# PEER routing tables: fused one-hot products, gates of 48 tiles applied from PSUM, split subtractions moved to GpSimd

## The reference

```python
q = (xn @ w_q).reshape(B, S, 8, 2, 64)
s = einsum('bshpd,hpkd->bshpk', q, sub_keys)          # 8 heads, 2 halves, 128 keys
v_half, i_half = top_k(s, 16)
top_s, top_c = top_k(v_half[..., 0, :, None] + v_half[..., 1, None, :], 16)
experts = i1 * 128 + i2                                # one of 16384, 128 per token
g = softmax(top_s)
act = gelu(einsum('cd,ced->ce', xc, expert_u[experts]))
y = einsum('ce,ced->cd', g * act, expert_v[experts])
```

## Time and profile before

| | us |
|---|---|
| median of 3 runs | 1444.72 |
| lowest, highest | 1444.61, 1446.04 |
| the profiled execution | 1441.05 |
| its span | 1439.2 |
| TensorE busy | 1253.0 (87%) |
| VectorE busy | 1091.7 (76%) |
| ScalarE busy | 720.3 (50%) |
| GpSimd busy | 683.8 (48%) |

### The profile page before, as it was taken

One profiled execution on the slowest core, in us unless ns is written; L12 is line 12 of the kernel. 1 busy time (PEld: TensorE's weight loads), 2 busy tenths in 40 slices (PEclk: granted clock), 3 DMA queues, 4 the chain that ended last, 5 costly groups with the idle time before them and its releaser, 6 DMA issues.

```text
span 1439.2 us, 27850 instructions
## 1 busy us (share of the span) xinstructions
PE 1253.0 (87%) x8802; PEld 1132.1 (79%) x8802; DVE 1091.7 (76%) x1727; ACT 720.3 (50%) x1473; POOL 683.8 (48%) x543
## 2 busy tenths in 40 slices
PE   7979989888978889899877777777899999999996
PEld 6978878777966889898876666666888878888785
DVE  4587777786355539994899999999568777788765
ACT  5435665434555455456433333333445555555554
POOL 2653543432356338999888888888630000000000
PEclk8999999998999999999999999999999999999999
DMA  5575655754534335454354545454777567766652
GB/s 209 169 227 188 204 185 186 249 160 170 206 105 144 112 110 174 156 167 162 121 160 143 159 146 160 146 159 147 234 257 253 190 245 250 249 245 205 236 191 100
DMA packets 98190, 261.92 MB, mean 182 GB/s; under 512 B 7979, under 2 KB 41899, under 8 KB 96844
## 3 DMA queue, kind: packets, MB, share of 16 engines
q1 hardware_dynamic: 90652, 232.76, 48.7%
q0 software_dynamic: 7472, 28.31, 5.8%
HBM read 241.65 MB, written 19.40 MB: 181 GB/s over the span
## 4 chain that ended last, share of the span: by engine, by line
PE 48%; DVE 25%; issue 11%; POOL 7%; ACT 4%; DMA 3%; DVEq 1%; POOLq 0%; ACTq 0%; SPq 0%
PE psum L640 47%; DVE w_lo L1530 8%; DVE arena L1930 7%; POOL w_lo L1400 5%; DVE s_sb L1927 3%; DVE s_sb L1539 2%; POOL arena L1466 2%; DMA ring<-v_rows 1%; ACT w_hi L1068 1%; DMA arena<-mods 1%; DVE arena L1928 1%; ACT arena L1205 1%; PE psum L803 1%; DVE arena L1759 1%; DVE rstd L1524 1%
## 5 line engine op out<-in xcount | busy, mean ns | idle before, releaser
L1068 ACT ACTIVATE w_hi<-ring 128x512 fp32r<-128x512 f32 x734 | 451.7, 629 | 494.5 <-PE psum L640 479.2
L640 PE MATMUL psum<-h_hi,w_hi 128*128 128x256 f32 x1832 | 542.9, 296 | 51.9 <-DVE w_lo L1530 19.6
L1400 POOL TENSOR_TENSOR w_lo<-ring,w_hi 128x512 fp32r<-128x512 f32 x287 | 421.0, 1476 | 279.5 <-ACT w_hi L1068 223.9
L640 PE MATMUL psum<-h_lo,w_hi 128*128 128x256 f32 x1832 | 523.0, 285 | 0.0
L640 PE MATMUL psum<-h_hi,w_lo 128*128 128x256 f32 x1832 | 522.3, 285 | 0.0
L640 PEld LDWEIGHTS psum<-h_hi,w_hi 128*128 128x128 f32 x1832 | 354.8, 194 | 73.4 <-issue 33.8
L1530 DVE TENSOR_TENSOR w_lo<-ring,w_hi 128x512 fp32r<-128x512 f32 x319 | 294.2, 923 | 122.4 <-ACT w_hi L1068 122.2
L640 PEld LDWEIGHTS psum<-h_lo,w_hi 128*128 128x128 f32 x1832 | 356.5, 195 | 0.3
L640 PEld LDWEIGHTS psum<-h_hi,w_lo 128*128 128x128 f32 x1832 | 355.7, 194 | 0.0
L640 PE MATMUL psum<-w_hi,h_hi 128*128 128x512 f32 (+1 forms) x592 | 223.8, 378 | 11.1 <-DVE arena L1547 5.4
L640 PE MATMUL psum<-w_lo,h_hi 128*128 128x512 f32 (+1 forms) x592 | 222.6, 376 | 0.0
(11 more groups left out here) (186 smaller groups left out, 1072.4 us busy)
## 6 DMA issues: line engine op xcount, KB each, us to landing
ring<-u_t SPq DMA_DIRECT2D x128, 512.0 KB, 3.5
ring<-v_rows SPq DMA_DIRECT2D x128, 512.0 KB, 3.5
ring<-weights SPq DMA_DIRECT2D x115, 512.0 KB, 3.7
arena<-mods POOLq DMA_DIRECT2D x48, 512.0 KB, 4.7
routing_weights<-s_sb SPq DMA_DIRECT2D x32, 512.0 KB, 4.8
s_sb<-routing_weights SPq DMA_DIRECT2D x8, 2048.0 KB, 9.2
bias_rows<-arena POOLq DMA_DIRECT2D x1, 1536.0 KB, 5.9
xres<-x_t SPq DMA_DIRECT2D x1, 1024.0 KB, 4.9
```

The lines of the kernel that those rows point to most:

```text
L640: return nc.tensor.matmul(out, lhs, rhs, start=start, stop=stop, **kw)
L1068: nc.scalar.activation(w_hi[:, half, :], src, ACT.Copy).then_inc(hi_done, 1)
L1400: nc.gpsimd.tensor_tensor(w_lo[:, half, :], src, w_hi[:, half, :].bitcast(F32), ALU.subtract)\
```

## The change

It rearranges the routing in four ways.

1. The table of quad q is cut in two. The part for tiles 0 to 47 never leaves PSUM: VectorE multiplies it straight into the 48 activations of these four tokens (`weigh_early`, 192 columns), after which ScalarE copies only the part of tiles 48 to 127 (`late_of`, 320 of 512 columns) to `stage`. HBM holds five groups instead of eight. The first product therefore uses only PSUM banks 0 and 1 in turn, and tile n waits for the gelu of tile n-2; the routing tables take banks 2, 3, 6, 7, as `sel_1` now stays in bank 4.
2. There is no `hot2` any more. The three weighted tables come from twelve `tensor_scalar` per quad on VectorE, each 128 columns: (iota == index) * piece, with both scalars read per partition from SBUF. The pieces are rounded to bf16 and kept as fp32 for that. `hot1` compares against an index column in PSUM.
3. GpSimd makes no tables; it does both low halves of all 128 tiles of the first product, and VectorE none.
4. VectorE's loop over quads is written out in full (64 times), and its weighings in the second product begin with tile 48, at other places of each group.

```diff
-UBANKS = (0, 1, 6, 7)
+UBANKS = (0, 1, 0, 1)
+GBANKS = (2, 3, 6, 7)
+XBANKS = (0, 1, 6, 7)
...
+LATE = (P - POOL_TILES) // GRP
...
-        hot1, hot2 = quads(flat(120, 2)), quads(s_sb[:, 0:512])
-        wgt = [quads(flat(122 + 2 * x, 2)) for x in range(3)]
-
-        sel_w = [s_sb[:, 512 + 128 * x:640 + 128 * x].bitcast(BF16) for x in range(3)]
-        rest = [s_sb[:, 1024 + T * x:1024 + T * x + T] for x in range(2)]
-        sel_1, sel_2 = std, rstd
-        stage = s_sb[:, 2048:4096].rearrange("p (b r t g) -> p b r t g", b=2, r=GROUPS, t=8)
+        hot1 = flat(112, 2).bitcast(BF16).rearrange("p (b t k) -> p b t k", b=2, t=4)
+        wgt = flat(114, 6).bitcast(BF16).rearrange("p (b t x k) -> p b t x k", b=2, t=4, x=3)
+        sel_2 = s_sb[:, 0:T]
+        sel_w = [s_sb[:, T * (x + 1):T * (x + 2)] for x in range(3)]
+        piece = s_sb[:, 1024:1024 + T // 2].bitcast(BF16)
+        rest = [s_sb[:, 1280 + T * x:1280 + T * x + T] for x in range(2)]
+
+
+        def late_of(bank):
+            return bank.rearrange("p (t r g) -> p t r g", t=4, r=GROUPS)[:, :, GROUPS - LATE:GROUPS, :]
+
+        def early_of(bank):
+            return bank.rearrange("p (t n) -> p n t", t=4)[:, 0:POOL_TILES, :]
+
+        stage = s_sb[:, 1024:1024 + 2 * LATE * 8 * GRP].rearrange("p (b r t g) -> p b r t g", b=2, r=LATE, t=8)
         g_back = s_sb[:, :].rearrange("p (t g) -> p g t", g=GRP)
...
-                    pe_.wait_ge(act_read, n - 3)
+                    pe_.wait_ge(act_read, n - 1)
...
             def quad(s, q, first):
                 pe_.wait_ge(hot1_ready, q + 1)
-                pe_.wait_ge(wgt0_ready, q + 1)
                 pe_.wait_ge(wgt_ready, q + 1)
                 if not first:
                     pe_.wait_ge(g_read, q - 3)
                 for j in range(4):
-                    out = psum[:, 2 + s, j * P:j * P + P]
                     for x in range(3):
-                        last = mm(out, hot1[:, s % 2, j, :], wgt[x][:, s % 2, j, :], x == 0, x == 2)
+                        last = nc.tensor.matmul(psum[:, GBANKS[s], j * P:j * P + P], hot1[:, s % 2, j, :], wgt[:, s % 2, j, x, :],
+                                                start=x == 0, stop=x == 2)
                 last.then_inc(route_done, 1)
...
-                act.wait_ge(route_done, q + 1)
+                act.wait_ge(early_weighted, q + 1)
                 dst = stage[:, s // 2, :, 4 * (s % 2):4 * (s % 2) + 4, :].rearrange("p r t g -> p t r g")
-                src = psum[:, 2 + s, :].rearrange("p (t r g) -> p t r g", t=4, r=GROUPS)
-                nc.scalar.activation(dst, src, ACT.Copy).then_inc(g_read, 1)
+                nc.scalar.activation(dst, late_of(psum[:, GBANKS[s], :]), ACT.Copy).then_inc(g_read, 1)
...
             def high_act(s, n, count, first):
-                act.wait_ge(weighted, count)
+                if count is not None:
+                    act.wait_ge(weighted, count)
                 if first:
-                    act.wait_ge(act_done, P)
+                    act.wait_ge(early_weighted, QUADS)
+                    act.wait_ge(half_used, NHALF + P)
                 else:
                     act.wait_ge(y_done, n - 3)
...
-            def low_tile(base, s, n, both):
-                src = ring[:, (NSLOT + base + s) % RING, :]
-                k = NSPLIT + base + s
-                if both:
-                    low(k, 2 * k % 4, src[:, 0:HSLOT], 2 * (NSPLIT + base + n) + 1, lo2_done)
-                else:
-                    pool.wait_ge(lo0_done, NSPLIT + base - POOL_TILES + n + 1)
-                low(k, (2 * k + 1) % 4, src[:, HSLOT:D], 2 * (NSPLIT + base + n) + 2, lo1_done)
-
-            with pool.Fori(0, POOL_TILES // 4) as it:
+            def low_tile(s, n):
+                src, k = ring[:, (NSLOT + s) % RING, :], NSPLIT + s
+                low(k, 2 * k % 4, src[:, 0:HSLOT], 2 * (NSPLIT + n) + 1, lo2_done)
+                low(k, (2 * k + 1) % 4, src[:, HSLOT:D], 2 * (NSPLIT + n) + 2, lo1_done)
+
+            with pool.Fori(0, P // 4) as it:
                 for s in range(4):
-                    low_tile(0, s, it * 4 + s, True)
-            with pool.Fori(POOL_TILES // 4, (POOL_TILES + QUADS) // 4) as it:
-                for s in range(4):
-                    low_tile(0, s, it * 4 + s, False)
-
-                    q = it * 4 + s - POOL_TILES
-                    pool.wait_ge(hot2_ready, q + 1)
-                    for x in (1, 2):
-                        w = sel_w[x][:, bass.ds(q * 4, 4)].unsqueeze(2).to_broadcast([P, 4, P])
-                        last = nc.gpsimd.tensor_tensor(wgt[x][:, s % 2, :, :], hot2[:, s % 2, :, :], w, ALU.mult)
-                    last.then_inc(wgt_ready, 1)
-            with pool.Fori((POOL_TILES + QUADS) // 4, P // 4) as it:
-                for s in range(4):
-                    low_tile(0, s, it * 4 + s, False)
+                    low_tile(s, it * 4 + s)
...
-            v.tensor_copy(sel_1[:, :], psum[:, 4, 0:T])
-            v.tensor_copy(sel_2[:, :], psum[:, 4, T:2 * T])
-            v.tensor_copy(sel_w[0], psum[:, 5, 0:T]).then_inc(sel_read, 1)
-            dve.wait_ge(sel_read, 1)
-            for x, whole in enumerate((psum[:, 5, 0:T], rest[0])):
-                v.tensor_tensor(rest[x], whole, sel_w[x], ALU.subtract).then_inc(sel_read, 1)
-                dve.wait_ge(sel_read, 2 * x + 2)
-                v.tensor_copy(sel_w[x + 1], rest[x]).then_inc(sel_read, 1)
-                dve.wait_ge(sel_read, 2 * x + 3)
-
-            def one_hots(s, q, first):
-                def of(x):
-                    return bc(x[:, bass.ds(q * 4, 4)].unsqueeze(2), [P, 4, P])
-
-                if not first:
+            v.tensor_copy(sel_2, psum[:, 4, T:2 * T]).then_inc(sel_read, 1)
+            whole = psum[:, 5, 0:T]
+            for x in range(3):
+                v.tensor_copy(piece, whole).then_inc(sel_read, 1)
+                dve.wait_ge(sel_read, 3 * x + 2)
+                v.tensor_copy(sel_w[x], piece).then_inc(sel_read, 1)
+                dve.wait_ge(sel_read, 3 * x + 3)
+                if x < 2:
+                    v.tensor_tensor(rest[x], whole, sel_w[x], ALU.subtract).then_inc(sel_read, 1)
+                    dve.wait_ge(sel_read, 3 * x + 4)
+                    whole = rest[x]
+
+            def one_hots(q):
+                if q >= 2:
                     dve.wait_ge(route_done, q - 1)
-                columns = bc(iota[:, :].unsqueeze(1), [P, 4, P])
-                v.tensor_tensor(hot2[:, s % 2, :, :], columns, of(sel_2), ALU.is_equal).then_inc(hot2_ready, 1)
-                v.tensor_tensor(hot1[:, s % 2, :, :], columns, of(sel_1), ALU.is_equal).then_inc(hot1_ready, 1)
-                dve.wait_ge(hot2_ready, q + 1)
-                v.tensor_tensor(wgt[0][:, s % 2, :, :], hot2[:, s % 2, :, :], of(sel_w[0]), ALU.mult)\
-                    .then_inc(wgt0_ready, 1)
-
-
-            for s in range(4):
-                low_u(s, POOL_TILES + s)
-                one_hots(s, s, s < 2)
-            with dve.Fori(POOL_TILES // 4 + 1, (POOL_TILES + QUADS) // 4) as it:
-                for s in range(4):
-                    low_u(s, it * 4 + s)
-                    one_hots(s, it * 4 + s - POOL_TILES, False)
-            with dve.Fori((POOL_TILES + QUADS) // 4, P // 4 - 2) as it:
-                for s in range(4):
-                    low_u(s, it * 4 + s)
+                rows = iota[:, :].unsqueeze(1).to_broadcast([P, 4, P])
+                v.tensor_tensor(hot1[:, q % 2, :, :], rows, bc(psum[:, 4, 4 * q:4 * q + 4].unsqueeze(2), [P, 4, P]), ALU.is_equal)\
+                    .then_inc(hot1_ready, 1)
+                for t in range(4):
+                    at = 4 * q + t
+                    for x in range(3):
+                        last = v.tensor_scalar(wgt[:, q % 2, t, x, :], iota[:, :], sel_2[:, at:at + 1], sel_w[x][:, at:at + 1],
+                                               ALU.is_equal, ALU.mult)
+                last.then_inc(wgt_ready, 1)
+
+            def weigh_early(q):
+                dve.wait_ge(route_done, q + 1)
+                if q == 0:
+                    dve.wait_ge(act_read, POOL_TILES)
+                a = arena[:, 0:POOL_TILES, 4 * q:4 * q + 4]
+                v.tensor_tensor(a, early_of(psum[:, GBANKS[q % 4], :]), a, ALU.mult).then_inc(early_weighted, 1)
+
+            for q in range(QUADS):
+                one_hots(q)
+                if q >= 1:
+                    weigh_early(q - 1)
+            weigh_early(QUADS - 1)
...
             def weigh(j, k):
                 dve.wait_ge(g_in, j * 16 + 16)
-                a = arena[:, bass.ds(j * GRP + 2 * k, 2), :]
+                a = arena[:, bass.ds(POOL_TILES + j * GRP + 2 * k, 2), :]
                 v.tensor_tensor(a, a, g_back[:, 2 * k:2 * k + 2, :], ALU.mult).then_inc(weighted, 1)
-
-            dve.wait_ge(act_read, GRP)
-            for k in range(GRP // 2):
-                low_u(k % 4, P - GRP // 2 + k)
-                weigh(0, k)
...
-            def low_group(j):
```

(45 more changed lines are left out.)

37 lines of the change are left out of this document (16 added, 21 removed).

## The result

The changed kernel takes 1515.55 us (median of 4 runs, 1509.42 to 1527.93), the kernel before 1444.66 (1443.83 to 1446.04) beside it: a ratio of 1.05, 95% interval 1.043 to 1.057. It is slower; 1422 was predicted. The profiled execution took 1509.42, with a span of 1507.6 (before: 1441.05 and 1439.2).

A forecast was written before the change was run, and what follows sets the result against it. It took the routing stretch to be bound by VectorE's and GpSimd's turns at their shared SBUF port. 1441.05 less 22 (routing) and 1 (second product) gave 1418, 3.7 more for the runs' median: 1422 us, range 1395 to 1506.

The forecast's parts named there:

- The bound before: Routing stretch: VectorE and GpSimd take turns at a shared SBUF port; turns sum to 5.15 of the 5.20 us period.
- the kind of the new operation: Routing, VectorE: tensor_scalar from SBUF also waits for GpSimd's whole turn, and itself holds the port only 0.09 us.
- The second scalar: Routing, the twelve tensor_scalar: 0.196 us from start to start with both scalar reads together, bounds 0.13 and 0.26.
- The place of the turns: Routing: GpSimd's first turn hits the end of the twelve, the second misses them; period about 4.7, taken as 4.85 us.
- Gate product and hot1: Routing, VectorE: with PSUM operands neither takes turns; gate product 0.40 us (bounds 0.28 to 0.5), hot1 0.60 start to start.
- Start of the stretch: Preparation before the first routing table: more operations take turns, but slack swallows them; 0, at worst 2 us.
- Two banks: First product: tile n waits for the gelu of n-2, about 1.0 us behind its tile, under 2.88 a tile: nothing.
- ScalarE's new wait: Routing: ScalarE's copy of a quad waits for VectorE's gate product, behind the next quad's tables, made long before: nothing.
- The second product: Fewer weighings and reloads save at most 1 us; each reload moving later on SP's queue costs nothing.
- (a): Rival, routing: both GpSimd turns fall inside the run of twelve; period 6.15 us, +60, 1505 us; chance 0.38.
- (b): Rival, routing: the twelve, at 0.13 us each, end before GpSimd asks; period 3.65 us, -97, 1347 us; chance 0.10.
- (c): Rival, routing: each turn costs a bit more, period 5.15 to 5.25 us, no measurable change; chance 0.04.

The follow-up runs named there:

- e5: The changed kernel with weighings behind tiles 4 to 11 and all tables as 512-column products, one input in PSUM: 1348.93 us, ratio 0.931 to the kernel before.
- e3: The changed kernel with the immediate 1.0 as second scalar of the twelve tensor_scalar, gate weights left out: 1463.32 us in one execution.
- e1: The changed kernel with the second product's eight weighings of a group back behind tiles 4 to 11: 1486.74 us, ratio 1.030 to the kernel before.
- e7: The kernel before with the eight weighings of a group behind tiles 4, 5, 7, 8, 10, 11, 13, 14: 1492.79 us in one execution.
- e2: The changed kernel with reloads 1 to 4 bringing 256 of 4096 columns, the other weights left out: 1489.24 us in one execution.
- e4: The changed kernel with the twelve tensor_scalar reading their column numbers from a copy in PSUM: 1443.80 us, ratio 0.999 to the kernel before.

## Why the prediction was wrong

**The bound before, and the kind of the new operation: right.** `tensor_scalar` from SBUF waits for GpSimd, up to 1.47 us long, as line 1872 had shown. That the 5.20 before were turns of the port rests on the sum of the turns. e5 fits it, with every operand pair kept off the port and the stretch at TensorE's floor, but it also gives GpSimd other work; no run changed the kernel before in this.

**The second scalar: the term that was mis-sized.** 0.196 was taken from a row with one scalar; it measures 0.256, the upper bound that the text gave. 12 x 0.06 = 0.72 per period. The price of the first scalar stood in two rows; that the second costs the same again was the likelier reading of them, as the row "of the same operation" has one scalar and not two.

**The place of the turns: the step that failed.** "The first turn falls on the last one or two of them ... just ahead of the second turn". The step let one of the two turns of a quad miss the twelve, also where it allowed the phase to slip (no turn in one period, two in the next, 4.9 in the mean). The runs show two in the mean, as every subtraction meets a run. e3 has exactly the 0.196 of this step and still a period of 5.02 instead of 4.7 to 4.95.

The step laid out the period by fixed distances from TensorE's small products. The trace shows no such steady period: the runs of twelve meet none to four turns, and the first six. In the rows shown, the four halves of two tiles come to GpSimd in one bunch and meet one run of twelve, as VectorE spends 3.2 of its 3.9 us in such a run. The sum that fits is VectorE's own work plus every turn: 3.94 + 1.83 = 5.77 with two scalars, 3.22 + 1.78 = 5.0 with one (measured 5.02). It is a sum of measured stalls, and what a turn costs was not known ahead. With the prediction's own 3.4 and its own 1.05 for a turn it gives 5.5, a slower kernel even before the second scalar's 0.72; with the measured 0.91 it gives 5.2, no change.

**Gate product and hot1: right in kind.** The gate product takes 0.27 from start to start, a little below the bounds (0.28 to 0.5), and hot1 0.60; neither stretches. The sum without stalls was 3.4 and is 3.94: + 0.72 for the scalar, - 0.13 for the gate product, - 0.06 for waits.

**Start of the stretch: nothing, as said.** The casts took turns, and the preparation lasted from 683.4 to 691.6, 8.3 us, within the 9.5 that the prediction allowed it. The first table began 2.0 us later than before, but the index transposes had ended 3.0 later already: 2.0 of that lies ahead of the first product, and 1.0 is the next point.

**Two banks: "nothing" was wrong by 1.0 us.** The step took the gelu to follow its tile by rounding and gelu, about 1.0, and left out ScalarE's table loads of 1.28. There TensorE waits 1.32 us for the gelu of n-2. Elsewhere it never does. The 15 tiles from 112 to 127 take 42.7 us in both kernels, as said.

**ScalarE's new wait: nothing, as said.** From 750 to 1050 us its copy (L1322) has no idle time before it.

**The second product: "half a group's weighings earlier than it is used: nothing" was false, and cost 30 us.** The step looked at when the reloaded table is needed, and not at what stands behind the reload on SP's queue. This is the second step that failed. The reload waits for the eighth weighing, which had moved from behind tile 11 to behind tile 14, while the ring covers four tiles: at 352.3 / 127 = 2.77 us a tile, three tiles are 8.3 us. e1 takes it away, e7 puts it into the old kernel. Fewer reloads, set at 1 us less, gained nothing that shows: 354.0 (e1) and 353.0 (e5) against 352.3.

**The rivals.** (a), with both turns inside the run, comes closest to the mechanism of the routing: two turns a quad in the mean, though not two in each run. Its period was set at 6.15, and is 5.77 (0.91 instead of 1.05 for a turn, and the smaller gate product). That its 1505 lies close to the measured 1515.55 is luck in part: its + 60 were + 36 in the routing, and the other 30 came from where no rival looked. Its condition, a start-to-start time above 0.23, was wrong too: at 0.196 the turns hit already. (b) needed 0.13; the twelve took 0.256, and 0.196 with one scalar. The formula of the Trainium skill ("VectorE: DVE Perf Modes", the section on the TRN2 errata) gives the same 0.13, by the prediction's estimate, so the earlier trace rows were nearer than the page. (c), no change, would have needed a period of 5.15 to 5.25.

**The clock.** TensorE's granted clock of 0.88 in tiles 48 to 112 goes with its waits for the tables. It adds no time of its own there: VectorE is busy without a gap, and its 3.94 of work and 1.83 of stalls are the whole period. Whether the slower TensorE shifts the bunches isn't tested.

**Still open:** why the bunches fall as they do (only their sum was tested), and how exactly the 30 us of the second product divide, as e2 is one execution and its two parts don't add up by themselves.

## What to carry to other kernels

When two engines share a port, price an operation by how often its neighbour's turns can hit it, and count every one of them, and first try to put one operand into PSUM: here slower instructions off the port beat faster ones on it (e4), and 512-column products with one operand in PSUM beat both (e5). When a wait on an in-order queue moves later, count what is queued behind it and compare the delay with the depth of the buffer that it fills. A period laid out by fixed distances is only as good as the proof that it repeats; else sum the turns over the whole stretch.
